# A hybrid decoder layer on one core: activation rows of 268 columns, other orders around two norms, three shifted feed-forward pairs

## The chip, the cores and the metric

The kernel runs on one core of one Trainium2 chip. The metric is the device time of one execution in microseconds. Work is shared by five engines, each with its own queue in program order: TensorE (PE; its weight loads are shown apart as PEld), VectorE (DVE), ScalarE (ACT), GpSimd (POOL) and SyncE (SP). They wait for each other on semaphores alone.

## The reference

One inference step of one decoder layer, for 256 prompt tokens and 8 sample tokens, 264 columns in all, in fp32:

```python
# token mixer: pooling branch, Mamba-2 SSD branch, gated merge, output projection
x = layer_norm(ALPHA * x + mix, ln_mix_g, ln_mix_b)
# cross-attention of 4 heads over 256 memory tokens
x = layer_norm(ALPHA * x + ca, ln_mem_g, ln_mem_b)
f = (silu(x @ w_ffn_gate) * (x @ w_ffn_up)) @ w_ffn_down      # 2048 -> 5632 -> 2048
x = layer_norm(ALPHA * x + f, ln_ffn_g, ln_ffn_b)

def layer_norm(x, g, b):
    mu = mean(x); var = mean((x - mu) ** 2)
    return (x - mu) * rsqrt(var + 1e-5) * g + b
```

It also returns the new SSD, convolution and pooling states and the memory keys and values.

## The kernel before

**Layout.** Activations are feature-major: a partition holds one feature of each of 16 tiles, and the columns are the 264 tokens. Every fp32 product is made of three matmuls on split operands: the rounded high part and the rest of the weights (`whi`, `wlo`) and of the activations (`xH`, `xL` for the layer's input `x`; `yH`/`yL`, `mixH`/`mixL`, `hH`/`hL` for the SSD output, the mixed branches and the hidden layer). `mm3` (L360 to L364) issues high x high (L362), high weights x low activations (L363) and low weights x high activations (L364).

**The weight stream.** All weights come as 688 units of 128 x 1024 fp32 (512 KB) through a ring of four slots. For each unit SP loads `raw` once the slot's last split is done, ACT's `split` writes `whi` (L807) once PE has finished the unit four before, DVE's `split` writes `wlo` (L1293) as `raw - whi`, and PE's `unit` waits for `wlo` and issues 24 matmuls: four tiles of the activations (`kk` 0 to 3), for each two output banks of three matmuls, so six matmuls in a row read the same tile. ACT and DVE can stand at most four units ahead of PE. Because every engine works in program order, a `split` that stands behind something that waits also waits, and so does PE's unit.

**Rows.** `xH` and `xL` hold 16 rows (one per tile) of T + 2 = 266 fp32 values in each partition, 1064 bytes from row to row; the two columns behind the 264 tokens are for the norm's gain and bias. `yH`, `mixH` and `hH` have rows of 264 values, 1056 bytes.

**The first norm** (`n` = 0, behind `w_out`). DVE adds the residual per block of two tiles (L1702, L1704), ACT squares it, DVE adds sums and squares, PE sums them over partitions (L601). Then for four chunks `c` of four tiles each: DVE's `ln_scale` (L1788, L1789: times the reciprocal deviation, plus the shifted mean), ACT's `ln_affine` (L1055, four activations: gain and bias), ACT's `ln_high` (L1062, writes `xH`), DVE's `ln_low` (L1793, writes `xL`). PE meanwhile makes the memory keys from `memH` (8 units, L623 and L624), and then the queries (8 units), which read `xH` and `xL` chunk by chunk.

**The second norm** (`n` = 1, behind `w_mo`, one unit per block of two tiles). Here the next matrix product starts before the norm's statistics are there: `gain_high` and `gain_low` write gain x residual into `xH` and `xL`, the first two feed-forward pairs run on these with 266 columns (the last two give the products with gain and bias), and DVE's `fix` (L1883, L1885) and `up_fixed` put deviation and mean in afterwards. A pair is one gate block and one up block of 4 units each, 8 units; there are 22 pairs. In the shadow of the two pairs DVE and ACT also make the true normed `x` (`ln_scale`, `ln_affine`), and write it over `xH` and `xL` (`ln_high`, `ln_low`) as PE leaves the chunks. Pairs 3 to 18 also carry the update of the sample states (`states`, `outers`).

**PSUM.** `SETS` are four pairs of banks: 0 and 1 are G, 2 and 3 are M. The blocks of `w_mo` go to sets 0, 1, 2 in turn; every pair has its gate in set 0 and its up in set 1. The sums of norm 1 use set 3.

## Time and profile before

| | |
|---|---|
| median of 3 runs | 2254.7 us (2253.25 to 2259.2) |
| the profiled execution's own time | 2259.79 us |
| its span | 2257.9 us |
| mean granted TensorE clock | 0.979 |
| PE busy | 2188.8 us, 97%, 17470 matmuls |
| PEld busy | 2161.8 us, 96% |
| DVE busy | 1465.7 us, 65% |
| ACT busy | 1138.8 us, 50% |
| POOL busy | 157.5 us, 7% |
| chain that ended last | PE 89%, DVE 6%, ACT 2%, DMA 2% |
| DMA | 451.75 MB, mean 200 GB/s |

The span runs from the first to the last instruction; 1.9 us of the profiled execution lie outside it. The busy share of PE counts matmuls whose spans overlap (a matmul takes about 0.29 us, and the next starts about 0.12 us after it), so what tells the pace is the distance from start to start. The clock of a stretch is the share of full speed that was granted: 1.00 is 2.4 GHz, and half of it 1.2 GHz.

### The profile page before, as it was taken

How to read it: one execution, taken by the hardware profiler on the slowest of the kernel's cores; microseconds unless marked ns; L12 is line 12 of the kernel's file. 1: busy time of each engine (PE TensorE's matmuls, PEld its weight loads, DVE VectorE, ACT ScalarE, POOL GpSimd, SP SyncE). 2: the span in 40 equal slices, each digit the busy share in tenths (PEclk: the TensorE clock that was granted, in tenths of full speed). 3: DMA queues.
4: the chain of work that ended last, by engine and by line, in shares of the span. 5: the costliest groups of instructions: out<-in, count | busy, mean ns of one | idle time of the engine just before them, and what ended most of it. 6: DMA issues, size and time to landing. Idle time of an engine off the chain costs nothing.

```text
span 2257.9 us, 47795 instructions
## 1 busy us (share of the span) xinstructions
PE 2188.8 (97%) x17470; PEld 2161.8 (96%) x17470; DVE 1465.7 (65%) x2336; ACT 1138.8 (50%) x1668; POOL 157.5 (7%) x295
## 2 busy tenths in 40 slices
PE   7999999999999998999999999989999999999995
PEld 6999999999999998999999999989999999999995
DVE  6688877888778887444446742876666665444444
ACT  4666566566545444343444542566656564443333
POOL 1000000000003331000000000001111110000000
PEclk9999999999999999999999987999999999999998
DMA  6555555455457997455556643358888886555552
GB/s 253 170 182 177 184 180 175 158 179 175 159 187 255 304 293 222 151 178 181 178 176 215 232 151 122 122 187 280 284 273 276 284 272 216 177 180 183 179 178 76
DMA packets 123104, 451.75 MB, mean 200 GB/s; under 512 B 15928, under 2 KB 16056, under 8 KB 121464
## 3 DMA queue, kind: packets, MB, share of 16 engines
q1 hardware_dynamic: 99648, 362.92, 46.6%
q0 software_dynamic: 23376, 87.69, 12.4%
q8 instruction: 59, 0.97, 0.2%
q14 instruction: 21, 0.17, 0.0%
HBM read 427.87 MB, written 23.99 MB: 200 GB/s over the span
## 4 chain that ended last, share of the span: by engine, by line
PE 89%; DVE 6%; ACT 2%; DMA 2%; issue 1%; SPq 0%; POOL 0%; DVEq 0%; ACTq 0%; POOLq 0%
PE G L362 24%; PE G L363 24%; PE G L364 24%; PE M L362 3%; PE M L363 3%; PE M L364 3%; DVE sb_wlo L1293 2%; DMA sb_raw<-in_wstream 1%; ACT sb_whi L807 1%; PE G L662 1%; PE M L449 1%; PE G L637 1%; PE M L459 1%; DVE sb_resid L1789 1%; DVE sb_resid L1788 1%
## 5 line engine op out<-in xcount | busy, mean ns | idle before, releaser
L1293 DVE TENSOR_TENSOR sb_wlo<-sb_raw,sb_whi 128x1024 fp32r<-128x1024 f32 x688 | 836.7, 1224 | 699.8 <-ACT sb_whi L807 698.6
L807 ACT ACTIVATE sb_whi<-sb_raw 128x1024 fp32r<-128x1024 f32 x688 | 723.1, 1058 | 809.5 <-PE G L364 662.2
L362 PE MATMUL G<-sb_xH,sb_whi 128*128 128x264 f32 (+1 forms) x3136 | 906.5, 289 | 29.3 <-DVE sb_wlo L1293 21.5
L363 PE MATMUL G<-sb_xL,sb_whi 128*128 128x264 f32 (+1 forms) x3136 | 902.7, 288 | 0.0
L364 PE MATMUL G<-sb_xH,sb_wlo 128*128 128x264 f32 (+1 forms) x3136 | 902.3, 288 | 0.0
L362 PEld LDWEIGHTS G<-sb_xH,sb_whi 128*128 128x128 f32 x3136 | 600.2, 191 | 36.6 <-issue 24.0
L363 PEld LDWEIGHTS G<-sb_xL,sb_whi 128*128 128x128 f32 x3136 | 599.5, 191 | 0.1
L364 PEld LDWEIGHTS G<-sb_xH,sb_wlo 128*128 128x128 f32 x3136 | 597.6, 191 | 0.0
L363 PE MATMUL G<-sb_hL,sb_whi 128*128 128x264 f32 x704 | 200.4, 285 | 0.0
L364 PE MATMUL G<-sb_hH,sb_wlo 128*128 128x264 f32 x704 | 200.1, 284 | 0.0
L362 PE MATMUL G<-sb_hH,sb_whi 128*128 128x264 f32 x704 | 199.5, 283 | 0.0
L362 PE MATMUL G<-sb_yH,sb_whi 128*128 128x264 f32 x512 | 146.8, 287 | 7.2 <-DVE sb_yL L1669 7.2
L363 PE MATMUL G<-sb_yL,sb_whi 128*128 128x264 f32 x512 | 146.9, 287 | 0.0
L364 PE MATMUL G<-sb_yH,sb_wlo 128*128 128x264 f32 x512 | 146.6, 286 | 0.0
L362 PEld LDWEIGHTS G<-sb_hH,sb_whi 128*128 128x128 f32 x704 | 132.6, 188 | 0.0
L364 PEld LDWEIGHTS G<-sb_hH,sb_wlo 128*128 128x128 f32 x704 | 132.5, 188 | 0.0
L363 PEld LDWEIGHTS G<-sb_hL,sb_whi 128*128 128x128 f32 x704 | 132.3, 188 | 0.0
L362 PE MATMUL M<-sb_xH,sb_whi 128*128 128x264 f32 x384 | 113.1, 295 | 4.0 <-DVE sb_xL L1793 4.0
L363 PE MATMUL M<-sb_xL,sb_whi 128*128 128x264 f32 x384 | 111.0, 289 | 0.0
L364 PE MATMUL M<-sb_xH,sb_wlo 128*128 128x264 f32 x384 | 111.0, 289 | 0.0
L362 PEld LDWEIGHTS G<-sb_yH,sb_whi 128*128 128x128 f32 x512 | 97.5, 190 | 7.3 <-issue 7.3
L364 PEld LDWEIGHTS G<-sb_yH,sb_wlo 128*128 128x128 f32 x512 | 97.2, 190 | 0.0
(355 smaller groups left out, 3002.0 us busy)
## 6 DMA issues: line engine op xcount, KB each, us to landing
sb_raw<-in_wstream SPq DMA_DIRECT2D x688, 512.0 KB, 3.5
sb_st<-in_state_ssd POOLq DMA_DIRECT2D x32, 512.0 KB, 6.1
out_new_ssd_s<-sb_st POOLq DMA_DIRECT2D x32, 512.0 KB, 3.3
sb_tmp<-in_state_ssd POOLq DMA_DIRECT2D x34, 256.0 KB, 5.1
sb_cumbc<-scr_cum POOLq DMA_DIRECT2D x8, 1024.0 KB, 4.9
...
```

The costliest lines, as they stand in the source:

```text
L362: pe.matmul(out, w, kH, start=start, stop=False)
L363: pe.matmul(out, w, kL, start=False, stop=False)
L364: return pe.matmul(out, wlo[:, slot, col:col + P], kH, start=False, stop=stop)
L449: pe.matmul(out, xdt[:, 0, h * 64:h * 64 + 64], MM[:, h % 3, 0:SEQ], start=True, stop=False)
L459: last = pe.matmul(M[2][:, j * P:j * P + P], xdt[:, b, j * P:j * P + P], Btok[:, b, :], start=b == 0, stop=b == 1)
L637: last = pe.matmul(X[:, c:c + 1], kc[:, h, b, m * P:m * P + P], qT[:, h, SEQ + b:SEQ + b + 1], start=True, stop=True)
L662: last = pe.matmul(X[:, 384 + c:385 + c], vc[:, h, b, m, :], sPT[:, m, c:c + 1], start=m == 0, stop=m == 1)
L807: act.activation(whi[:, slot, :], raw[:, slot, :], ACT.Copy).then_inc(hi_ready, 1)
L1293: dve.tensor_tensor(wlo[:, slot, :], raw[:, slot, :], whi[:, slot, :].bitcast(F32), ALU.subtract)\
L1788: step(dve.tensor_tensor(chunk(c), chunk(c), spread(RSTD[n]), ALU.mult))
L1789: dve.tensor_tensor(chunk(c), chunk(c), spread(MEAN[n]), ALU.add).then_inc(s["zn_ready"], 1)
```

## The change

Four things. (1) `xH` and `xL` get rows of T + 4 = 268 values, 1072 bytes; the small table `rc` moves into an overlay to make room. (2) First norm: DVE does three of the last block's four splits ahead of its residual instead of four, and the first `ln_scale` to `ln_low` are put in another order among the splits; ACT does the first chunk's affine and high part before the first keys. (3) Second norm: the first pair has its gate in set 2 and its up in set 0, the second in sets 1 and 2, and a third pair runs on the shifted residual in sets 0 and 1; the sums over partitions come behind the first gate's fourth unit instead of the third; DVE leaves the last tiles' sums and the last squares until after the last gain. (4) `ln_scale`, `ln_affine`, `ln_high` and `ln_low` of the second norm are spread over three pairs instead of two, so that one pair fewer follows the states.

The diff, without its parts that only change the signatures of `columns`, `fix` and `up_fixed` (each gets the pair of banks as an argument):

```diff
-        xH = alloc(ctx, "xH", [P, KT, T + 2], F32R)
-        xL = alloc(ctx, "xL", [P, KT, T + 2], F32R)
+        xH = alloc(ctx, "xH", [P, KT, T + 4], F32R)
+        xL = alloc(ctx, "xL", [P, KT, T + 4], F32R)
...
-        rc = alloc(ctx, "rc", [P, 4, 16])
+        (rc,) = overlay(KEEP + 3 * XPG * SG * 4 + 3 * P * 4, rc=([P, 4, 16],))
...
-            def pair(between=None, **kw):
+            def pair(gate, up, ready=None, between=None, n=T):
 
                 pe.wait_ge(s["sgm"], START["sgm"] + t["sgm"].now())
-                block_units(xH, xL, KT, SETS[0], between=between, **kw)
-                kw.pop("before", None)
+                block_units(xH, xL, KT, SETS[gate], n=n, before=ready, between=between)
                 pe.wait_ge(s["h_read"], START["h_read"] + t["h_read"].now())
-                block_units(xH, xL, KT, SETS[1], **kw)
+                block_units(xH, xL, KT, SETS[up], n=n)
                 t["sgm"].add(2)
                 t["h_read"].add(2)
 
-            pe.wait_ge(s["res_ready"], 8 + 7)
-            pair(n=T + 2, before=lambda q: pe.wait_ge(s["gd_lo"], 4 * (q + 1)), between=lambda q: ln_folded(1) if q == 2 else None)
-            pair(n=T + 2)
-            with rounds(pe, FT // 2 - 2, t, dict(unit=8, sgm=2, h_read=2)):
-                pair(before=lambda q: pe.wait_ge(s["x_lo"], 8 + q + 1))
+            pe.wait_ge(s["res_ready"], 8 + 6)
+            pair(2, 0, n=T + 2, ready=lambda q: pe.wait_ge(s["gd_lo"], 4 * (q + 1)),
+                 between=lambda q: ln_folded(1) if q == 3 else None)
+            pair(1, 2, n=T + 2)
+            pe.wait_ge(s["h_read"], START["h_read"] + 2)
+            pair(0, 1, n=T + 2)
+            with rounds(pe, FT // 2 - 3, t, dict(unit=8, sgm=2, h_read=2)):
+                pair(0, 1, ready=lambda q: pe.wait_ge(s["x_lo"], 8 + q + 1))
...
             ln_squares(0, 7)
-            split(2)
+            split(1)
             ln_mean(0)
             split(1)
             ln_sd(0)
             split(1)
+            ln_affine(0, 0)
+            ln_high(0, 0)
+            split(1)
             keys(0)
-            for c in range(4):
+            for c in (1, 2, 3):
                 ln_affine(0, c)
                 ln_high(0, c)
-                split(1)
+                split(1 if c < 3 else 2)
             keys(1)
...
+            split(4)
+            ln_mean(1)
+            ln_sd(1)
+            columns(0, 2)
+            split(1)
+            silu_fixed(0)
+            split(1)
+            ln_affine(1, 0)
             split(2)
-            ln_mean(1)
-            split(1)
-            ln_sd(1)
-            columns(0)
-            split(1)
-            silu_fixed(0)
-            ln_affine(1, 0)
-            split(1)
+            columns(1, 0)
+            hidden_high()
+
+            split(2)
             ln_affine(1, 1)
             split(2)
-            columns(1)
-            split(1)
+            ln_affine(1, 2)
+            columns(0, 1)
+            split(1)
+            silu_fixed(1)
+            split(3)
+            ln_affine(1, 3)
+            columns(1, 2)
             hidden_high()
 
-            split(2)
-            ln_affine(1, 2)
-            split(2)
-            columns(0)
-            silu_fixed(1)
-            ln_affine(1, 3)
+            split(4)
+            columns(0, 0)
+            silu_fixed(2)
             for c in range(4):
                 split(1)
                 act.wait_ge(used, t["done"].now() + c + 1 + RING)
                 ln_high(1, c)
-            columns(1)
+            columns(1, 1)
             hidden_high()
 
...
-                split(4)
+                split(4 if b < 7 else 3)
...
             ln_rstd(0)
             ln_scale(0, 0)
             split(1)
-            for c in range(4):
-                if c < 3:
-                    ln_scale(0, c + 1)
-                split(1)
-                ln_low(0, c)
+            ln_scale(0, 1)
+            split(1)
+            ln_low(0, 0)
+            split(1)
+            ln_scale(0, 2)
+            ln_low(0, 1)
+            split(1)
+            ln_scale(0, 3)
+            ln_low(0, 2)
+            split(2)
+            ln_low(0, 3)
             split(8)
...
-                if b:
+                if 0 < b < 7:
                     add_tiles(1, b)
-                if b >= 2:
+                if 2 <= b < 7:
                     add_squares(1, b - 1)
                 if b:
                     gain_low(b - 1)
+            gain_low(7)
+            split(1)
+            add_tiles(1, 7)
+            add_squares(1, 6)
             add_squares(1, 7)
-            gain_low(7)
             fold(1)
 
...
             ln_variance(1)
             split(1)
             ln_rstd(1)
-            split(1)
-            fix(0, sgF)
+            fix(0, 2, sgF)
+            split(1)
             ln_scale(1, 0)
+            split(3)
+            up_fixed(0)
+            hidden_low()
+
             split(1)
             ln_scale(1, 1)
-            split(3)
-            up_fixed()
-            hidden_low()
-
             split(2)
             ln_scale(1, 2)
-            split(2)
-            fix(0, sgF)
+            split(1)
+            fix(0, 1, sgF)
+            split(1)
             ln_scale(1, 3)
+            split(3)
+            up_fixed(2)
+            hidden_low()
+
+            split(4)
+            fix(0, 0, sgF)
             for c in range(4):
                 split(1)
                 if c == 3:
-                    up_fixed()
+                    up_fixed(1)
                 ln_low(1, c)
             hidden_low()
 
```

What stands where, before and after. In these rows `sb_wlo` is a split of DVE, `sb_resid<-sb_resid,sb_lrstd` and `sb_resid<-sb_resid,sb_mean` are the two halves of `ln_scale`, and `sb_xL<-sb_resid,sb_xH` is `ln_low`.

DVE in the first norm, from the scale of chunk 1 to the low part of chunk 2, before:

```order
L1788 TENSOR_TENSOR sb_resid<-sb_resid,sb_lrstd 128x1056
L1789 TENSOR_TENSOR sb_resid<-sb_resid,sb_mean 128x1056
L1293 TENSOR_TENSOR sb_wlo<-sb_raw,sb_whi 128x1024
L1793 TENSOR_TENSOR sb_xL<-sb_resid,sb_xH 128x4x264
L1788 TENSOR_TENSOR sb_resid<-sb_resid,sb_lrstd 128x1056
L1789 TENSOR_TENSOR sb_resid<-sb_resid,sb_mean 128x1056
L1293 TENSOR_TENSOR sb_wlo<-sb_raw,sb_whi 128x1024
L1793 TENSOR_TENSOR sb_xL<-sb_resid,sb_xH 128x4x264
L1788 TENSOR_TENSOR sb_resid<-sb_resid,sb_lrstd 128x1056
L1789 TENSOR_TENSOR sb_resid<-sb_resid,sb_mean 128x1056
L1293 TENSOR_TENSOR sb_wlo<-sb_raw,sb_whi 128x1024
L1793 TENSOR_TENSOR sb_xL<-sb_resid,sb_xH 128x4x264
```

The same stretch of DVE after the change:

```order
L1799 TENSOR_TENSOR sb_resid<-sb_resid,sb_lrstd 128x1056
L1800 TENSOR_TENSOR sb_resid<-sb_resid,sb_mean 128x1056
L1304 TENSOR_TENSOR sb_wlo<-sb_raw,sb_whi 128x1024
L1804 TENSOR_TENSOR sb_xL<-sb_resid,sb_xH 128x4x264
L1304 TENSOR_TENSOR sb_wlo<-sb_raw,sb_whi 128x1024
L1799 TENSOR_TENSOR sb_resid<-sb_resid,sb_lrstd 128x1056
L1800 TENSOR_TENSOR sb_resid<-sb_resid,sb_mean 128x1056
L1804 TENSOR_TENSOR sb_xL<-sb_resid,sb_xH 128x4x264
L1304 TENSOR_TENSOR sb_wlo<-sb_raw,sb_whi 128x1024
L1799 TENSOR_TENSOR sb_resid<-sb_resid,sb_lrstd 128x1056
L1800 TENSOR_TENSOR sb_resid<-sb_resid,sb_mean 128x1056
L1804 TENSOR_TENSOR sb_xL<-sb_resid,sb_xH 128x4x264
```

Counting the units of the stream from the first of the memory keys as 0, the two splits shown first are units 8 and 9 before and 7 and 8 after: unit 8 now stands between the low part of chunk 0 and the scale of chunk 2, and unit 9 between the low part of chunk 1 and the scale of chunk 3.

ACT from the standard deviation of the first norm to the high part of chunk 1 (`sb_KTm` are keys, `sb_resid<-sb_resid,sb_vec` is the affine, `sb_xH` the high part), before:

```order
L1045 ACTIVATE sb_lrstd<-sb_lrstd,sb_eps 128x264
L807 ACTIVATE sb_whi<-sb_raw 128x1024
L1083 ACTIVATE sb_KTm<-G 128x256 x2
L1055 ACTIVATE sb_resid<-sb_resid,sb_vec 128x264 x4
L1062 ACTIVATE sb_xH<-sb_resid 128x4x264
L807 ACTIVATE sb_whi<-sb_raw 128x1024
L1055 ACTIVATE sb_resid<-sb_resid,sb_vec 128x264 x4
L1062 ACTIVATE sb_xH<-sb_resid 128x4x264
```

And after:

```order
L1047 ACTIVATE sb_lrstd<-sb_lrstd,sb_eps 128x264
L809 ACTIVATE sb_whi<-sb_raw 128x1024
L1057 ACTIVATE sb_resid<-sb_resid,sb_vec 128x264 x4
L1064 ACTIVATE sb_xH<-sb_resid 128x4x264
L809 ACTIVATE sb_whi<-sb_raw 128x1024
L1085 ACTIVATE sb_KTm<-G 128x256 x2
L1057 ACTIVATE sb_resid<-sb_resid,sb_vec 128x264 x4
L1064 ACTIVATE sb_xH<-sb_resid 128x4x264
```

The keys come after the first chunk. The two splits shown are units 7 and 8 before, and 6 and 7 after: each unit from 8 on now stands behind the high part of one chunk later (unit 8 behind chunk 1, unit 9 behind chunk 2, units 10 and 11 behind chunk 3), where before it stood behind chunks 0, 1, 2 and 3.

DVE at the end of the blocks of `w_mo`, from the last block's residual on (`sb_xL<-sb_resid,sb_vec,sb_xH` is `gain_low`, `sb_sums` are the sums of tiles and squares), before:

```order
L1707 SCALAR_TENSOR_TENSOR sb_resid<-sb_resid,G 128x528
L1729 TENSOR_TENSOR sb_sums<-sb_sums,sb_resid 128x528
L1741 TENSOR_TENSOR sb_sums<-sb_sums,sb_squares 128x528
L1853 SCALAR_TENSOR_TENSOR sb_xL<-sb_resid,sb_vec,sb_xH 128x264 x2
L1741 TENSOR_TENSOR sb_sums<-sb_sums,sb_squares 128x528
L1853 SCALAR_TENSOR_TENSOR sb_xL<-sb_resid,sb_vec,sb_xH 128x264 x2
L1748 TENSOR_TENSOR sb_sums<-sb_sums 128x264 x2
L1293 TENSOR_TENSOR sb_wlo<-sb_raw,sb_whi 128x1024 x2
```

And after:

```order
L1718 SCALAR_TENSOR_TENSOR sb_resid<-sb_resid,G 128x528
L1870 SCALAR_TENSOR_TENSOR sb_xL<-sb_resid,sb_vec,sb_xH 128x264 x4
L1304 TENSOR_TENSOR sb_wlo<-sb_raw,sb_whi 128x1024
L1740 TENSOR_TENSOR sb_sums<-sb_sums,sb_resid 128x528
L1752 TENSOR_TENSOR sb_sums<-sb_sums,sb_squares 128x528 x2
L1759 TENSOR_TENSOR sb_sums<-sb_sums 128x264 x2
L1304 TENSOR_TENSOR sb_wlo<-sb_raw,sb_whi 128x1024 x2
```

The gains and one split stand ahead of the last sums.

## Rows read from the trace of the kernel before

**Rows 1.** The page's first line.

```profile
span 2257.9 us, 47795 instructions
```

**Rows 2.** What PE waited for, 1275:1315 us: us in total, times, longest.

```profile
PE M L362 <- DVE sb_xL L1793: 4.0, 3, 1.6
PE G L601 <- DVE sb_sums L1748: 0.8, 1, 0.8
```

**Rows 3.** The same view, 1410:1512 us.

```profile
PE G L362 <- DVE sb_xL L1793: 3.9, 1, 3.9
PE G L362 <- DVE sb_resid L1707: 3.8, 1, 3.8
PE G L362 <- DVE sb_wlo L1293: 3.3, 1, 3.3
```

**Rows 4.** Windows: busy (x instructions) of PE, PEld, DVE, ACT, POOL; clock; DMA, GB/s.

```profile
1530.00:1700.00 170.00, 170.00 (x1384) 170.00 (x1383) 113.74 (x199) 102.00 (x199) 23.57 (x44) 1.00 0.82 278
1970.00:2100.00 130.00, 130.00 (x1072) 129.93 (x1070) 60.32 (x56) 50.16 (x52) 0.00 (x0) 1.00 0.54 180
```

**Rows 5.** Windows, instructions that touch `sb_xH` alone, whole span (no POOL).

```profile
0.00:2258.00 2258.00, 1336.05 (x7040) 1118.31 (x7040) 28.09 (x38) 20.60 (x30) 0.98 0.59 200
```

**Rows 6.** Timeline of PE: start, us; each sixth matmul, rows 6 to 11.

```profile
1610.04 0.29 PE L362 MATMUL G<-sb_xH,sb_whi 128*128 128x264 f32 x1
...
1610.79 0.28 PE L362 MATMUL G<-sb_xH,sb_whi 128*128 128x264 f32 x1
...
1611.53 0.28 PE L362 MATMUL G<-sb_xH,sb_whi 128*128 128x264 f32 x1
...
1612.24 0.28 PE L362 MATMUL G<-sb_xH,sb_whi 128*128 128x264 f32 x1
...
1612.99 0.29 PE L362 MATMUL G<-sb_xH,sb_whi 128*128 128x264 f32 x1
...
1613.72 0.29 PE L362 MATMUL G<-sb_xH,sb_whi 128*128 128x264 f32 x1
...
1614.46 0.28 PE L362 MATMUL G<-sb_xH,sb_whi 128*128 128x264 f32 x1
```

**Rows 7.** Timeline of DVE in the first norm, one round.

```profile
1299.28 1.22 DVE L1293 TENSOR_TENSOR sb_wlo<-sb_raw,sb_whi 128x1024 fp32r<-128x1024 f32 x1
1300.42 1.25 DVE L1793 TENSOR_TENSOR sb_xL<-sb_resid,sb_xH 128x1056 fp32r<-128x1056 f32 x1
1301.58 1.25 DVE L1788 TENSOR_TENSOR sb_resid<-sb_resid,sb_lrstd 128x1056 f32<-128x1056 f32 x1
1302.87 1.26 DVE L1789 TENSOR_TENSOR sb_resid<-sb_resid,sb_mean 128x1056 f32<-128x1056 f32 x1
1304.05 1.22 DVE L1293 TENSOR_TENSOR sb_wlo<-sb_raw,sb_whi 128x1024 fp32r<-128x1024 f32 x1
```

**Rows 8.** Timeline of ACT there.

```profile
1299.40 2.10 ACT L1055 ACTIVATE sb_resid<-sb_resid,sb_vec 128x264 f32<-128x264 f32 x4 [0.86 <-DVE sb_resid L1789]
1301.53 1.09 ACT L1062 ACTIVATE sb_xH<-sb_resid 128x1056 fp32r<-128x1056 f32 x1
1302.53 1.04 ACT L807 ACTIVATE sb_whi<-sb_raw 128x1024 fp32r<-128x1024 f32 x1
```

**Rows 9.** Windows at two of the second norm's stalls, columns as in rows 4.

```profile
1436.00:1444.00 8.00, 6.47 (x30) 6.47 (x31) 7.93 (x13) 3.60 (x7) 0.00 (x0) 0.57 0.39 131
1470.00:1475.00 5.00, 3.58 (x18) 3.58 (x19) 4.83 (x6) 2.05 (x4) 0.00 (x0) 0.66 0.44 132
```

**Rows 10.** Timeline of DVE and ACT at the last two blocks of `w_mo`.

```profile
1436.78 0.70 DVE L1707 SCALAR_TENSOR_TENSOR sb_resid<-sb_resid,G 128x528 f32<-128x528 f32 x1
...
1440.70 0.70 DVE L1707 SCALAR_TENSOR_TENSOR sb_resid<-sb_resid,G 128x528 f32<-128x528 f32 x1
...
1441.43 0.64 ACT L1036 ACTIVATE sb_squares<-sb_resid 128x528 f32<-128x528 f32 x1 [2.47 <-DVE sb_resid L1707]
1441.98 0.91 ACT L1164 ACTIVATE sb_xH<-sb_resid,sb_vec 128x264 fp32r<-128x264 f32 x2
...
1444.11 0.89 DVE L1853 SCALAR_TENSOR_TENSOR sb_xL<-sb_resid,sb_vec,sb_xH 128x264 fp32r<-128x264 f32 x2
```

18 lines of the change are left out of this document (9 added, 9 removed).

## The prediction

> **What bounds the kernel now.** I read four views. The page first: the span is 2257.9 us [rows 1], and its chain of waits lies mostly in PE's own matmuls, so the time is the sum of PE's steps and its stalls. Next, what PE waited for, by stretch. Two of the stretches with stalls are where the order changes: in the first norm PE stands idle 4.0 us in three waits for low parts of `x` and 0.8 us for the sums [rows 2]; in the second 3.9, 3.8 and 3.3 us, one wait each, for the low part of chunk 0, for the last-but-one residual and for a weight split [rows 3], 11.0 us in all. Then the windows for the pace: where PE never stalls and reads `xH` and `xL`, 1384 matmuls fill 170 us, 122.8 ns each; over the hidden layer, 1072 fill 130 us, 121.3 ns [rows 4]. Last, the timeline of both norms, for what each wait waits on.
>
> **Rows of 1072 bytes.** The change adds no matmul; it moves where a row of `xH` and `xL` begins. With three arrays of 16,384 bytes ahead of them, row k begins at 1064k bytes: even rows on a multiple of 16, odd rows 8 bytes off. In one stall-free stretch each row is read by six matmuls. Rows 6 to 11 take, start to start, 0.75, 0.74, 0.71, 0.75, 0.73 and 0.74 us [rows 6]: the even ones 0.730 on average, the odd ones 0.743, or 121.7 and 123.9 ns per matmul. That is one sample at a resolution of 10 ns, but the pace of the hidden layer, all of whose rows are multiples of 32 bytes, points the same way. At 1072 bytes every row begins on a multiple of 16. Two estimates: half the matmuls lose 2.2 ns, 1.1 ns on average; or all fall to the hidden layer's pace, 1.5 ns. The even rows of 1064 are not alike themselves: row 6, 48 bytes past a multiple of 64, takes 0.75, as slow as any odd row, and with 1072 a quarter of the rows begin so instead of an eighth. I take 0.85 ns. `xH` is read by 7040 matmuls [rows 5], two of every three, so 10,560 are touched: 10,560 x 0.85 ns = 9.0 us less. The bounds are 10,560 x 1.5 = 15.8 us less, and nothing. DVE and ACT touch `xH` in 38 and 30 instructions in all [rows 5]; a few ns in these don't reach PE.
>
> The Trainium skill bears on this from both sides. Its page "SBUF — State Buffer" (Specifications (TRN2)) gives 16-byte cachelines, with a penalty for each crossing to a new line; a row of 264 fp32 values that begins 8 bytes off crosses one line more. The page "TensorE: Matmul & The Clock Gate" (Back-to-back issue gap) sets the spacing of a stream by the matmul's columns and the weight load together, with no word of where a row begins; by it the pace would not change, which is the first rival below. The difference between rows 6 to 11 leans to the first page.
>
> **The first norm.** What goes: DVE no longer does the fourth split ahead of the last residual, so the sums come about a split (1.1 us) earlier, and the 0.8 us wait for them [rows 2] ends. What is late next is the splits of units 8 to 10 of the stream, counted from the first of the memory keys; units 8 to 11 are the first queries. Before, ACT split unit 8 behind chunk 0, 9 behind chunk 1, 10 behind chunk 2, and the scale of chunk 1 was done before DVE came to unit 8, so a round was bounded by DVE alone: one unit every 4.77 us (1299.28 to 1304.05) [rows 7]. PE needs 2.96 us for a unit (24 x 123 ns), which leaves a wait of some 1.3 us behind each. After, ACT's split of unit 9 stands behind the affine and high part of chunk 2, these wait for DVE's scale of chunk 2, and that stands behind DVE's split of unit 8, which itself waits for ACT behind chunk 1. So a round is a chain with no overlap: DVE's split 1.14 (1299.28 to 1300.42), scale 1.29 + 1.26 = 2.55 [rows 7], ACT's affine 2.13, high part 1.00, split 1.04 [rows 8], and a few hand-overs of some 0.05: 7.95 us. It occurs twice, for units 9 and 10; unit 11 follows unit 10 at once. PE waits 7.95 - 2.96 = 5.0 us twice, and about 0.4 at unit 8, since that split now follows chunk 1. New stalls 10.4, old 4.0 + 0.8: 5.6 us more, and I take 5.5. Behind the waiting splits on DVE stand the low parts of chunks 1 and 2; those are later too, but within the same waits.
>
> Such stalls cost clock besides. In the second norm, behind stalls of 3.3 to 3.9 us, the granted clock is 0.57 over 8 us and 0.66 over 5 us, part of the time at 1.2 GHz [rows 9], which loses 8 x 0.43 = 3.4 us and 5 x 0.34 = 1.7 us against 2.4 GHz. Stalls of up to 1.6 us in the first norm show no such thing. Behind the first 5.0 us stall the loss is hidden: a unit at half clock takes at most 2 x 2.96 = 5.9 us and the chain 7.95. Behind the second it is not: 1.7 to 3.4, I take 2.5. The bounds of this part: if the chain overlapped after all, 0.8 less than before; if both stalls cost 3.4 us of clock in the open, 5.6 + 6.8 = 12.4 more.
>
> **The second norm.** Three stalls of 11.0 us [rows 3] and three losses of clock, 3.4 + 1.7 + 1.7 (the third stall's window reads like the second's) = 6.8 us; 17.8 us is all there is.
> The wait for the residual (3.8): PE's first gate goes to set 2, free since the residual of block 5. DVE's residuals come 3.92 us apart (1436.78, 1440.70) [rows 10], so that of block 5 began at about 1432.9, and PE starts the gate about 3.7 us sooner, at 1433.8. Its fourth unit needs the last gain: the last residual stays at 1440.7, ACT squares it at 1441.43 (0.64 from issue) and makes the gain's high part from 1441.98 (0.91), DVE's low part takes 0.89 and stands ahead of everything else now, so it ends at 1443.8 instead of 1445.0 [rows 10]. PE has done three units by 1433.8 + 8.9 = 1442.7: it waits 1.2. The sums' tail on DVE (split 1.1, tiles 0.6, two squares 1.2, fold 0.7) ends at 1447.4, and the fourth unit at 1446.9: 0.6.
> The wait for the split (3.3): it came from a scale, an affine and a split in turn between ACT and DVE inside one pair. Now two or more splits stand between such chains everywhere but ahead of the third pair, where DVE's scale of chunk 3 (2.5 us) stands before its second unit: 0.3 + 0.65 there.
> The wait for the low part (3.9): the last scale and affine were done only as PE left the chunk. With a third pair they lie a pair earlier, and high and low parts of chunks 0 to 3 take 3.4 us a chunk between the two engines against PE's 2.96 per unit, started 6 us ahead: no wait.
> What is left is 1.2 + 0.6 + 0.95 = 2.8 us. A third pair with 266 columns instead of 264 costs 192 matmuls x 1 ns = 0.2. So 17.8 - 2.8 - 0.2 = 14.8 us less. If 1.2 and 0.6, so close together, cost a window of clock (1.7 us), 13.1; I allow half of that, 0.8. Bounds: 11, if another wait of the old size (3.8) comes in place of one, and 17.8.
>
> **The rest** costs nothing: `rc` is read in the pooling stage, which is loaded long before; a pair fewer behind the states leaves three, 72 us, for their last stores, which PE never waits for; the tail and the attention stage are the same.
>
> **The sum**, against the profiled execution's own 2259.8 us (its span 2257.9 and 1.9 around it): -9.0 + 5.5 + 2.5 - 14.8 + 0.8 = -15.0, so 2244.8. The median is 2254.7, 5.1 below that execution, so 2239.7; I say 2240.
>
> **The rivals.** (a) The row's start buys nothing: the 2.2 ns between odd and even rows would be their place in the unit, which doesn't change. For it: row 6 is as slow as the odd ones. Against it: the pace over the hidden layer is 1.5 ns better with the same places. The time: 2240 + 9 = 2249. (b) No chain in the first norm, because ACT comes through earlier than I reckon: 5.5 + 2.5 + 0.8 less, 2231. For it: ACT's first chunk stands ahead of the keys now. Against it: the order of both queues. (c) The second norm keeps one stall of the old size with its clock, at the third or fourth pair: 3.8 + 1.7 more, 2245. (d) Slower: what sets the pace is not 16 bytes but how a row lies in 64, or the distance between rows, and 1072 is the worse one. The slowest rows now take 0.75 us for six, 125 ns, 2.2 more than the pace of 122.8; if all did, 10,560 x 2.2 = 23.2 us more, and with the norms as above 2254.7 + 23.2 + 5.5 + 2.5 - 14 = 2272. It decides, with a kernel over 0.3% slower, from 12.8 us lost on, a pace of 124.0. For it: row 6. Against it: rows 8 and 10, at 0 and 16 bytes past, with 0.71 and 0.73 [rows 6].
>
> **How the numbers follow.** My forecast 70%, with 2232 to 2247 as its own range; (a) 12%, (b) 8%, (c) 6%, (d) 4%. The range that holds 8 in 10 is 2230 to 2249. A measurement of this kernel can tell 0.3%, 6.8 us, from no change: faster means below 2247.9. All of (b) and (c), nearly all of the forecast and a fifth of (a) lie there: 86%; within 0.3% most of (a) and the forecast's upper edge, 10%; slower (d), 4%.
>
> **What would show it.** The pace over `xH` near 122.0 ns in the window of 170 us (about 1393 matmuls where 1384 were), and no difference left between odd and even rows; the pace over the hidden layer as before. In the first norm two waits of PE for `sb_wlo`, near 5 us each, with the clock below 1 behind the second. In the second norm no wait over 1.5 us. Wrong would be: a pace over `xH` still at 122.8; waits in the first norm of 2 us or less; a wait over 3 us for `sb_xL` or `sb_wlo` in the pairs.

## The result, and the profile after

| | before | after |
|---|---|---|
| median | 2254.42 us (2253.25 to 2259.2, 4 runs) | 2227.95 us (2226.09 to 2229.49, 4 runs) |
| profiled execution | 2259.79 us | 2226.51 us |
| span | 2257.9 us | 2225.0 us |

The changed kernel is faster by 26.5 us, a ratio of 0.9878 [0.9861, 0.9896]. The forecast was 2240 with a range down to 2230: the direction came as written and so did what happens in both norms, the size did not, and the time fell below the range. The two profiled executions lie 33.0 us of span apart, more than the medians, because the one of before was about 5 us above its median and the one of after 1.4 below. Two single executions, one of 3531 us with only `xL` at 1072 bytes and one of 2653 us with the first norm alone, fell far out of their kernels' spread at a much lower granted clock and are left out of the medians and ratios below.

The page of after, its first line, the busy times and the chain that ended last (the line that answers to [rows 1] is the first):

```profile
span 2225.0 us, 47769 instructions
...
PE 2159.8 (97%) x17470; PEld 2133.2 (96%) x17470; DVE 1469.3 (66%) x2342; ACT 1138.6 (51%) x1670; POOL 157.4 (7%) x295
...
PE 89%; DVE 5%; DMA 2%; ACT 2%; issue 1%; SPq 0%; POOL 0%; DVEq 0%; ACTq 0%; POOLq 0%
```

PE's matmuls are as many as before and still make the chain. To see where 33.0 us went, I took from PE's timeline of both kernels the start of certain units of the weight stream (us; unit 392 is the first of the memory keys, 404 the fifth of the queries, 416 the first of `w_mo`, 424 the first of pair 0, 448 the first of pair 3, 600 the first of `w_ffn_down`):

| stretch | before | after | difference |
|---|---|---|---|
| start to 392, no edit but the rows | 1272.36 | 1260.09 | -12.3 |
| 392 to 404, first norm | 41.52 | 46.59 | +5.1 |
| 404 to 416, queries 5 to 8, values, attention | 92.07 | 89.26 | -2.8 |
| 416 to 448, `w_mo` and three pairs | 116.97 | 101.21 | -15.8 |
| 448 to 600, nineteen pairs | 448.90 | 441.81 | -7.1 |
| 600 to the end | 286.12 | 286.02 | -0.1 |

One profile of each kernel is not exact to a microsecond or two in such a stretch: the time at 1.2 GHz in the first row, for one, is 17.1 us before and 13.7 after. The repeat of the changed kernel below shows how far it moves.

**The pace.** Windows of after over the stretches of [rows 4]; the columns are the same:

```profile
1530.00:1700.00 170.00, 170.00 (x1406) 170.00 (x1406) 115.06 (x208) 104.93 (x209) 23.23 (x44) 1.00 0.83 281
1970.00:2100.00 130.00, 130.00 (x1071) 129.93 (x1070) 60.81 (x55) 48.57 (x48) 0.00 (x0) 1.00 0.54 180
```

In 170 us without a stall 1406 matmuls stand where 1384 were; 1393 were forecast. Over the hidden layer, whose rows weren't touched, nothing moves: 1071 against 1072. Sixteen pairs without a stall (units 456 to 584, 3072 matmuls) give the sharper number: 378.02 us before, 372.05 after, which is 123.05 and 121.11 ns per matmul, 1.94 ns less. The timeline of PE, each sixth matmul, answers to [rows 6]:

```profile
1610.49 0.28 PE L362 MATMUL G<-sb_xH,sb_whi 128*128 128x264 f32 x1
...
1611.22 0.29 PE L362 MATMUL G<-sb_xH,sb_whi 128*128 128x264 f32 x1
...
1611.95 0.28 PE L362 MATMUL G<-sb_xH,sb_whi 128*128 128x264 f32 x1
...
1612.68 0.29 PE L362 MATMUL G<-sb_xH,sb_whi 128*128 128x264 f32 x1
```

The three rows shown take 0.73 us each, where odd and even ones took 0.74 and 0.73 on average before, with single ones from 0.71 to 0.75. Over the same sixteen pairs, each row read 32 times: even rows took 122.0 ns per matmul before and 121.1 after, odd rows 124.1 and 121.1. Single rows still differ after the change, from 119.4 ns (row 3) to 124.2 (row 2), though all begin on a multiple of 16. This pattern over the 16 rows is the same to 0.1 ns in all seven profiles with rows of 1072 bytes, and another one is the same in all four with 1064.

**The first norm.** What PE waited for, 1265:1320 us of after, against [rows 2]:

```profile
PE M L362 <- DVE sb_wlo L1304: 9.0, 3, 4.8
```

Three waits, 9.0 us, where 4.8 were. The timeline of PE has each of them:

```profile
1284.94 0.36 PE L362 MATMUL M<-sb_xH,sb_whi 128*128 128x264 f32 x1 [0.77 <-DVE sb_wlo L1304]
...
1292.85 0.56 PE L362 MATMUL M<-sb_xH,sb_whi 128*128 128x264 f32 x1 [4.77 <-DVE sb_wlo L1304]
...
1300.77 0.36 PE L362 MATMUL M<-sb_xH,sb_whi 128*128 128x264 f32 x1 [3.47 <-DVE sb_wlo L1304]
```

They stand 7.91 and 7.92 us apart, start to start. Why, the timelines of DVE and then of ACT say (a bracket is the idle time ahead of the instruction and who ended it):

```profile
1283.56 1.23 DVE L1304 TENSOR_TENSOR sb_wlo<-sb_raw,sb_whi 128x1024 fp32r<-128x1024 f32 x1 [2.20 <-ACT sb_whi L809]
1284.71 1.25 DVE L1799 TENSOR_TENSOR sb_resid<-sb_resid,sb_lrstd 128x1056 f32<-128x1056 f32 x1
1285.99 1.26 DVE L1800 TENSOR_TENSOR sb_resid<-sb_resid,sb_mean 128x1056 f32<-128x1056 f32 x1
1287.17 1.25 DVE L1804 TENSOR_TENSOR sb_xL<-sb_resid,sb_xH 128x1056 fp32r<-128x1056 f32 x1
1291.48 1.23 DVE L1304 TENSOR_TENSOR sb_wlo<-sb_raw,sb_whi 128x1024 fp32r<-128x1024 f32 x1 [3.06 <-ACT sb_whi L809]
```

```profile
1287.29 2.10 ACT L1057 ACTIVATE sb_resid<-sb_resid,sb_vec 128x264 f32<-128x264 f32 x4 [3.75 <-DVE sb_resid L1800]
1289.42 1.08 ACT L1064 ACTIVATE sb_xH<-sb_resid 128x1056 fp32r<-128x1056 f32 x1
1290.41 1.04 ACT L809 ACTIVATE sb_whi<-sb_raw 128x1024 fp32r<-128x1024 f32 x1
```

Read across both: split on DVE, its two scales, then ACT's affine (idle 3.75 us until then), high part and split, then DVE again (idle 3.06 us until then). Neither engine does anything beside the other but one low part. From one split to the next it is 1283.56 to 1291.48, 7.92 us; [rows 7, 8] had given 7.95.

**The second norm.** What PE waited for, 1400:1512 us of after, against 11.0 us in [rows 3]:

```profile
PE M L601 <- DVE sb_sums L1759: 1.0, 1, 1.0
PE M L362 <- DVE sb_xL L1870: 0.5, 1, 0.5
PE G L362 <- DVE sb_wlo L1304: 0.3, 1, 0.3
PE M L572 <- DVE sb_resid L1718: 0.2, 1, 0.2
```

And the windows: the clock behind the first norm's long wait, the attention, and the whole of the second norm.

```profile
1290.00:1296.00 6.00, 3.15 (x15) 3.18 (x16) 4.48 (x4) 2.25 (x4) 0.00 (x0) 0.72 0.25 86
...
1330.11:1395.94 65.83, 64.85 (x439) 62.61 (x437) 19.90 (x38) 20.77 (x46) 1.59 (x3) 0.82 0.39 133
1410.00:1512.00 102.00, 100.12 (x803) 99.03 (x802) 88.40 (x115) 62.70 (x100) 2.12 (x4) 1.00 0.53 174
```

Over the second norm the granted clock is 1.00 throughout, where [rows 9] had 0.57 and 0.66.

### The profile page after: what moved, and what is told of

It is laid out like the page before. It is cut to its first block, busy times and chain, and to the rows that moved or that the text cites. A ratio compares the mean times of both kernels' runs of the same rounds, so it can differ in the third digit from the quotient of the medians.

```text
span 2225.0 us, 47769 instructions
## 1 busy us (share of the span) xinstructions
PE 2159.8 (97%) x17470; PEld 2133.2 (96%) x17470; DVE 1469.3 (66%) x2342; ACT 1138.6 (51%) x1670; POOL 157.4 (7%) x295
## 4 chain that ended last, share of the span: by engine, by line
PE 89%; DVE 5%; DMA 2%; ACT 2%; issue 1%; SPq 0%; POOL 0%; DVEq 0%; ACTq 0%; POOLq 0%
PE G L362 24%; PE G L363 24%; PE G L364 24%; PE M L362 3%; PE M L363 3%; PE M L364 3%; DVE sb_wlo L1304 2%; DMA sb_raw<-in_wstream 2%; PE M L449 1%; ACT sb_whi L809 1%; PE G L662 1%; PE G L637 1%; PE M L459 1%; ACT sb_resid L1057 1%; DVE sb_resid L1800 0%
## 5 line engine op out<-in xcount | busy, mean ns | idle before, releaser
L362 PE MATMUL G<-sb_xH,sb_whi 128*128 128x264 f32 (+1 forms) x3072 | 880.5, 287 | 19.9 <-DVE sb_wlo L1304 19.9
L364 PE MATMUL G<-sb_xH,sb_wlo 128*128 128x264 f32 (+1 forms) x3072 | 875.7, 285 | 0.0
L363 PE MATMUL G<-sb_xL,sb_whi 128*128 128x264 f32 (+1 forms) x3072 | 875.4, 285 | 0.0
L362 PEld LDWEIGHTS G<-sb_xH,sb_whi 128*128 128x128 f32 x3072 | 581.9, 189 | 26.8 <-issue 20.7
L363 PEld LDWEIGHTS G<-sb_xL,sb_whi 128*128 128x128 f32 x3072 | 581.6, 189 | 0.1
L364 PEld LDWEIGHTS G<-sb_xH,sb_wlo 128*128 128x128 f32 x3072 | 581.3, 189 | 0.0
L363 PE MATMUL G<-sb_hL,sb_whi 128*128 128x264 f32 x704 | 200.4, 285 | 0.0
L364 PE MATMUL G<-sb_hH,sb_wlo 128*128 128x264 f32 x704 | 200.0, 284 | 0.0
L362 PE MATMUL G<-sb_hH,sb_whi 128*128 128x264 f32 x704 | 199.5, 283 | 0.0
L362 PE MATMUL G<-sb_yH,sb_whi 128*128 128x264 f32 x512 | 146.6, 286 | 7.2 <-DVE sb_yL L1680 7.2
L363 PE MATMUL G<-sb_yL,sb_whi 128*128 128x264 f32 x512 | 146.6, 286 | 0.0
L364 PE MATMUL G<-sb_yH,sb_wlo 128*128 128x264 f32 x512 | 146.3, 286 | 0.0
L362 PE MATMUL M<-sb_xH,sb_whi 128*128 128x264 f32 (+1 forms) x448 | 132.1, 295 | 9.5 <-DVE sb_wlo L1304 9.0
L362 PEld LDWEIGHTS G<-sb_hH,sb_whi 128*128 128x128 f32 x704 | 132.6, 188 | 0.0
L364 PEld LDWEIGHTS G<-sb_hH,sb_wlo 128*128 128x128 f32 x704 | 132.5, 188 | 0.0
L363 PEld LDWEIGHTS G<-sb_hL,sb_whi 128*128 128x128 f32 x704 | 132.2, 188 | 0.0
L363 PE MATMUL M<-sb_xL,sb_whi 128*128 128x264 f32 (+1 forms) x448 | 129.8, 290 | 0.0
L364 PE MATMUL M<-sb_xH,sb_wlo 128*128 128x264 f32 (+1 forms) x448 | 129.7, 289 | 0.0
L362 PEld LDWEIGHTS G<-sb_yH,sb_whi 128*128 128x128 f32 x512 | 97.4, 190 | 7.3 <-issue 7.3
L362 PEld LDWEIGHTS M<-sb_xH,sb_whi 128*128 128x128 f32 x448 | 87.0, 194 | 10.8 <-issue 9.5
```

The lines of the kernel that those rows point to most:

```text
L362: pe.matmul(out, w, kH, start=start, stop=False)
L363: pe.matmul(out, w, kL, start=False, stop=False)
L364: return pe.matmul(out, wlo[:, slot, col:col + P], kH, start=False, stop=stop)
```

## The experiments

The question after the result was: does the row's start give twice what I took, or does something else in the change give it? And do the other two parts cost and give what their rows say? Each part was done alone and undone alone.

**Rows alone.** Kernel before, with rows of 1072 bytes and `rc` moved, as in the change.

```diff
-        xH = alloc(ctx, "xH", [P, KT, T + 2], F32R)
-        xL = alloc(ctx, "xL", [P, KT, T + 2], F32R)
+        xH = alloc(ctx, "xH", [P, KT, T + 4], F32R)
+        xL = alloc(ctx, "xL", [P, KT, T + 4], F32R)
-        rc = alloc(ctx, "rc", [P, 4, 16])
+        (rc,) = overlay(KEEP + 3 * XPG * SG * 4 + 3 * P * 4, rc=([P, 4, 16],))
```

> The kernel before with nothing changed but the rows of xH and xL (268 columns, 1072 bytes) and the place of rc. Theory A: the start of a row on a multiple of 16 bytes sets the pace; in the changed kernel the pace over xH was 121.4 ns where it was 122.95, so 10,560 x 1.55 ns = 16.4 us less than before (2238), about 1406 matmuls in the window 1530:1700 instead of 1384, and the waits of both norms as before (4.0 + 0.8 and 11.0 us). Theory B (my prediction's size): 0.85 ns, 9 us less (2245.5). Rival: the pace fell because of something else in the changed kernel (fewer stalls, other transfers), then 2254 and 122.9 ns here.

Measured: 2239.65 us (2235.36 to 2240.87) against 2257.72 of the kernel before on the same chip, ratio 0.9918 [0.9897, 0.9939], which is 18.5 us (13.8 to 23.3). The window of 170 us:

```profile
1530.00:1700.00 170.00, 170.00 (x1406) 170.00 (x1405) 114.07 (x204) 104.13 (x206) 23.54 (x44) 1.00 0.83 283
```

The full 1406 matmuls are there, and the stalls of both norms are those of before. So the rows alone give 18.5 us, about two thirds of the whole gain, and my 9.0 falls.

**Rows back.** Kernel after, rows of 1064 bytes again.

```diff
-        xH = alloc(ctx, "xH", [P, KT, T + 4], F32R)
-        xL = alloc(ctx, "xL", [P, KT, T + 4], F32R)
+        xH = alloc(ctx, "xH", [P, KT, T + 2], F32R)
+        xL = alloc(ctx, "xL", [P, KT, T + 2], F32R)
```

> The changed kernel with rows of 266 columns again, all else as changed. Theory A: the pace returns to 122.9 ns over xH and the time rises by 16 us over the changed kernel, to about 2244; even and odd rows differ by 2 ns again. Theory B: 9 us, 2237. The stalls of both norms stay as in the changed kernel (9 us and 2 us).

Measured: 2246.17 us (2242.83 to 2250.25), ratio 0.9952 [0.9936, 0.9968]: against the changed kernel's 0.9878 that is 0.0074, some 17 us. (`rc` stays where the change put it, so its move isn't what gives the time.) Its window:

```profile
1530.00:1700.00 170.00, 170.00 (x1384) 170.00 (x1383) 112.38 (x198) 102.51 (x202) 23.64 (x44) 1.00 0.83 278
```

1384 matmuls again. Done or undone, the part is worth the same within the noise, so it does not depend on the rest.

**Rows of 1068 bytes.** Kernel after. Row k then begins 0, 12, 8 or 4 bytes past a multiple of 16, in turn.

```diff
-        xH = alloc(ctx, "xH", [P, KT, T + 4], F32R)
-        xL = alloc(ctx, "xL", [P, KT, T + 4], F32R)
+        xH = alloc(ctx, "xH", [P, KT, T + 3], F32R)
+        xL = alloc(ctx, "xL", [P, KT, T + 3], F32R)
```

> The changed kernel with rows of 267 columns, 1068 bytes: only every fourth row begins on a multiple of 16, the others 4, 8 or 12 bytes off. Theory A (each row off a multiple of 16 costs its six matmuls about 3.9 ns each, from 1.94 ns on average at half the rows off): three quarters off, 121.1 + 2.9 = 124.0 ns over xH, 10,560 x 2.9 = 31 us over the changed kernel, 2259. Rival 1 (only 8 bytes off costs): a quarter off, 122.1 ns, 10 us over. Rival 2 (it is the pitch of 1064 bytes and not the row's start): 121.1 ns and no change.

Measured: 2247.56 us (2244.79 to 2250.76), ratio 0.996 [0.9947, 0.9974], some 21 us slower than the changed kernel in the same session (its repeat below).

```profile
1530.00:1700.00 170.00, 170.00 (x1388) 170.00 (x1387) 111.77 (x199) 101.95 (x199) 23.48 (x44) 1.00 0.82 278
```

1388 in the window; 122.71 ns per matmul over the sixteen pairs, where I had written 124.0, 122.1 or 121.1: none of the three came. A count of rows off 16 would have made it worse than 1064 (three of four off instead of one of two), and it is a shade better. By row, from PE's timeline over the same pairs, the means are 122.3 ns at 0 bytes, 120.7 at 12, 124.2 at 8 and 123.7 at 4. In the changed kernel, with all of them aligned, the same rows take 121.0, 121.6, 121.2 and 120.6. So rows 8 and 4 bytes off are slower by 3 ns, the aligned ones by 1.3, and rows 12 off are faster by 0.9. Which row is 12 off is also always the second tile of a unit; but that place isn't a fast one, it is the slowest of the four when all are aligned. What these means can't show is which matmul a cost belongs to, if it comes out in a neighbour, and each is of four rows only, where single aligned rows differ by up to 4.8 ns. The Trainium skill ("SBUF — State Buffer", Specifications (TRN2)) counts a penalty for each crossing into a new 16-byte cacheline; a row of 1056 bytes crosses one line more at any start that isn't a multiple of 16. The trace agrees for 4 and 8 bytes (123.7 and 124.2 against 122.3 ns) and not for 12 (120.7).

**Only `xL` at 1072 bytes.** Kernel after, `xH` at 1064.

```diff
-        xH = alloc(ctx, "xH", [P, KT, T + 4], F32R)
+        xH = alloc(ctx, "xH", [P, KT, T + 2], F32R)
```

> The changed kernel with xH at 266 columns again and only xL at 268: one matmul in three reads aligned rows. Theory A (each read of a row off a multiple of 16 pays for itself): the changed kernel gains 1.94 ns per matmul over the pitch of 1064, so a third of it is left, 122.4 ns over xH and 12 us over the changed kernel. Rival (the cost arises between two reads, from one row's start to the next one's, so that a mixed order is no better): 123.0 ns, 18 to 20 us over.

Measured: 2237.6 us (2234.97 to 2241.05) against 2258.83, ratio 0.99 [0.9885, 0.9915], by the ratios 5 to 7 us slower than the changed kernel.

```profile
1530.00:1700.00 170.00, 170.00 (x1396) 170.00 (x1395) 114.26 (x204) 103.25 (x206) 23.56 (x44) 1.00 0.83 280
```

The pace is 121.94 ns, so 1.11 of the 1.94 ns are won, 57%, where only one matmul in three reads `xL`. It meets neither expectation: a saving of an equal share for each matmul that reads an aligned row would be a third. Either a matmul of `xL` gains 3.3 ns itself, or one beside it gains with it. PE's timeline tells: each product is issued as `xH`, `xL`, `xH` (L362, L363, L364), and from the start of each to the next start the means over the sixteen pairs are

| from the start of | before | only `xL` | changed |
|---|---|---|---|
| L362, reads `xH` | 122.6 | 122.6 | 121.1 |
| L363, reads `xL` | 123.0 | 121.4 | 120.9 |
| L364, reads `xH` | 123.5 | 121.8 | 121.4 |

With only `xL` aligned, the matmul that reads it gains 1.6 ns and the one behind it 1.7, though that one still reads `xH` as before; the one ahead of it gains nothing. So what `xL` costs off 16 comes out in two matmuls, the reader and the next. Why, no run shows.

**First norm put back.** Kernel after, with ACT's and DVE's old orders in the first norm.

```diff
-            split(1)
+            split(2)
...
-            ln_affine(0, 0)
-            ln_high(0, 0)
-            split(1)
...
-            for c in (1, 2, 3):
+            for c in range(4):
...
-                split(1 if c < 3 else 2)
+                split(1)
...
-                split(4 if b < 7 else 3)
+                split(4)
...
-            ln_scale(0, 1)
-            split(1)
-            ln_low(0, 0)
-            split(1)
-            ln_scale(0, 2)
-            ln_low(0, 1)
-            split(1)
-            ln_scale(0, 3)
-            ln_low(0, 2)
-            split(2)
-            ln_low(0, 3)
+            for c in range(4):
+                if c < 3:
+                    ln_scale(0, c + 1)
+                split(1)
+                ln_low(0, c)
```

> The changed kernel with the first norm's orders on ACT and DVE as before (four splits ahead of the last residual, keys ahead of the first chunk, one scale, split and low part in turn). Theory A (the chain of scale, affine, high part, split and split costs 5.6 us less 0.5, and some clock behind it): the waits for wlo in the first norm (4.8 + 3.5 + 0.8) go, three waits for xL of 1.1 to 1.6 us come back, the queries start 5 us earlier, and the time is 5 to 8 us under the changed kernel, about 2222. Rival: the attention stage is held by something else (transfers, its own clock), and the time stays within 2 us of 2228.

Measured: 2225.81 us (2221.98 to 2228.69), ratio 0.9856 [0.9835, 0.9876], by the ratios 5 us under the changed kernel (0.9878) and 3 under its repeat (0.987), with intervals that overlap both. What PE waited for is [rows 2] again:

```profile
PE M L362 <- DVE sb_xL L1801: 4.0, 3, 1.6
PE G L601 <- DVE sb_sums L1756: 0.8, 1, 0.8
```

The stretch 392 to 404 takes 41.5 us, 5.1 less than in the changed kernel. But the next, 404 to 416, takes 93.5 instead of 89.3. So the waits behave as I said, and part of what they cost comes back in the next stretch.

**First norm alone.** Kernel before, with the new orders; in ACT's queue (and DVE's, as in the change):

```diff
-            split(2)
+            split(1)
...
+            ln_affine(0, 0)
+            ln_high(0, 0)
+            split(1)
...
-            for c in range(4):
+            for c in (1, 2, 3):
...
-                split(1)
+                split(1 if c < 3 else 2)
```

> The kernel before with the first norm's part of the change alone. Theory A: two waits for wlo of about 4.7 us, 392 to 404 takes 47 to 49 us instead of 41.5, and the attention stage behind it gives back about 3 us, because less of it falls to 1.2 GHz: 2 to 4 us over the kernel before, hardly to be told from no change. Rival: the attention stage gives nothing back, 6 to 8 us over it.

Measured: 2262.1 us (2259.58 to 2265.95) against 2258.83, ratio 1.0017 [1.0008, 1.0027], 3.8 us slower (1.8 to 6.1).

```profile
PE M L362 <- DVE sb_wlo L1296: 8.2, 3, 4.7
```

8.2 us of waits in place of 4.8, and 392 to 404 takes 48.8 us, 7.3 more; 404 to 416 takes 85.7, 6.3 less than in the profile of before. This part costs, but less than its waits.

**The changed kernel again**, with no edit.

> The changed kernel once more, beside the next three on one chip. All theories: 26 to 30 us under the kernel before. In its profile unit 392 to 404 of the stream (the first norm) 46.6 us, 416 to 448 (the second) 101 us; the attention stage between them, 404 to 416, anything from 85 to 94 us, by where the stretches at 1.2 GHz fall, if these differ from execution to execution (theory A); or 89.3 us again, if they are fixed by the kernel (rival).

Measured: 2226.32 us (2224.98 to 2233.26) against 2257.11, ratio 0.987 [0.9853, 0.9887], which is 29 us where the first comparison had 26.5. Its profile gives 48.9 us for 392 to 404 and 91.3 for 404 to 416, where the first gave 46.6 and 89.3. One kernel, two profiles, 2 us apart in each stretch. Windows of the attention (units 408 to 416), in three fences: of before, of the first norm alone, and of this run.

```profile
1335.87:1405.95 70.08, 69.10 (x438) 66.81 (x437) 19.90 (x38) 20.76 (x46) 1.59 (x3) 0.76 0.37 131
```

```profile
1340.64:1407.42 66.78, 65.81 (x438) 63.50 (x437) 19.90 (x38) 20.75 (x46) 1.59 (x3) 0.80 0.42 146
```

```profile
1329.51:1398.95 69.44, 68.46 (x438) 65.90 (x437) 19.90 (x38) 20.78 (x46) 1.59 (x3) 0.76 0.38 132
```

The work is the same to the instruction. Time multiplied by clock: 70.08 x 0.76 = 53.3, 66.78 x 0.80 = 53.4, 69.44 x 0.76 = 52.8, and in the window of after above 65.83 x 0.82 = 54.0. What differs is the share of the stretch at 1.2 GHz. Summed over 404 to 416, the time at 1.2 GHz is 40.8 us in the profile of before, 34.1 in that of after, 39.5 in this run, 44.5 with the first norm put back and 26.9 with the first norm alone.

**ACT's splits ahead of the affine.** Kernel after; in ACT's queue alone each split of the first norm moves from behind a chunk's affine and high part to ahead of it.

```diff
-            split(1)
+            split(2)
             ln_affine(0, 0)
...
             for c in (1, 2, 3):
+                split(1)
                 ln_affine(0, c)
                 ln_high(0, c)
-                split(1 if c < 3 else 2)
```

> The changed kernel with DVE's order untouched and one split of ACT moved: two splits ahead of the first chunk's affine, and the others ahead of their chunk instead of behind it. Theory A (each split on ACT that stood behind a chunk's high part waited for DVE's scale, which stood behind DVE's split of the unit before): the chain opens, one wait of about 1 us for wlo is left of 9, and the time is 8 to 10 us under the changed kernel, about 2219. Rival: DVE's order alone (a split ahead of the scales of chunks 2 and 3) makes the chain; then the waits of 4.8 and 3.5 us stay and the time is 2228.

Measured: 2220.58 us (2218.99 to 2222.18), ratio 0.9838 [0.9821, 0.9855]. PE's waits in the first norm:

```profile
PE M L362 <- DVE sb_wlo L1304: 2.3, 1, 2.3
```

And ACT's timeline in place of the one above:

```profile
1285.36 1.06 ACT L809 ACTIVATE sb_whi<-sb_raw 128x1024 fp32r<-128x1024 f32 x1
1286.31 2.10 ACT L1057 ACTIVATE sb_resid<-sb_resid,sb_vec 128x264 f32<-128x264 f32 x4
1288.44 1.09 ACT L1064 ACTIVATE sb_xH<-sb_resid 128x1056 fp32r<-128x1056 f32 x1
1289.43 1.04 ACT L809 ACTIVATE sb_whi<-sb_raw 128x1024 fp32r<-128x1024 f32 x1
```

The affine has no idle time before it, where it had 3.75 us. DVE's order is that of the changed kernel. So moving ACT's splits is enough to open the chain, and DVE's order alone doesn't make it. No run put DVE's order back and left ACT's, so whether that would open it too isn't shown.

**The same kernel once more**, beside the runs of other parts on another chip.

> The changed kernel with one split of ACT moved ahead, once more: 2219 to 2221, 36 us under the kernel before, about 6 to 8 under the changed one. If its lead was an accident of where the slow clock fell, 2226.

Measured: 2223.85 us (2220.62 to 2224.55) against 2258.83, ratio 0.984 [0.9826, 0.9853]. Of the kernels here it is the fastest: 1.6% under the kernel before both times, and by the ratios 7 to 9 us under the changed one (0.9838 and 0.984 against 0.9878 and 0.987). Its two profiles lie as far apart as any: 404 to 416 takes 85.4 us in the first and 91.5 in the second, with 26.6 and 39.8 us of it at 1.2 GHz.

**Second norm alone.** Kernel before, with that part of the change only: the same edits as in the diff ahead of the prediction (sets, third shifted pair, late sums, the spread of scales and affines), rows of 1064 bytes, first norm as before; only `rc` is moved as well.

```diff
-            pair(n=T + 2, before=lambda q: pe.wait_ge(s["gd_lo"], 4 * (q + 1)), between=lambda q: ln_folded(1) if q == 2 else None)
-            pair(n=T + 2)
...
+            pair(2, 0, n=T + 2, ready=lambda q: pe.wait_ge(s["gd_lo"], 4 * (q + 1)),
+                 between=lambda q: ln_folded(1) if q == 3 else None)
+            pair(1, 2, n=T + 2)
+            pe.wait_ge(s["h_read"], START["h_read"] + 2)
+            pair(0, 1, n=T + 2)
```

> The kernel before with the second norm's part of the change alone (set rotation, third pair, late sums; rows of 266 columns, first norm as before). Theory A: 416 to 448 takes 103 us where the kernel before takes 117, and the time is 13 to 15 us under the kernel before. Rival: the gain is only there together with the shorter rows' pace, under 8 us.

Measured: 2245.79 us (2242.79 to 2245.96), ratio 0.9949 [0.9935, 0.9962], 11.5 us less (8.6 to 14.7). Its stretch 416 to 448 takes 102.8 us where the profile of before had 117.0, and the clock is 1.00 over the norm itself (3.6 us at 1.2 GHz lie ahead of it, in the first blocks of `w_mo`):

```profile
1420.00:1506.00 86.00, 84.08 (x671) 83.09 (x671) 75.83 (x99) 53.06 (x83) 0.00 (x0) 1.00 0.50 170
```

**Two shifted pairs.** Kernel after without the third pair, with the sets' rotation and the late sums kept.

```diff
-            pe.wait_ge(s["h_read"], START["h_read"] + 2)
-            pair(0, 1, n=T + 2)
-            with rounds(pe, FT // 2 - 3, t, dict(unit=8, sgm=2, h_read=2)):
+            with rounds(pe, FT // 2 - 2, t, dict(unit=8, sgm=2, h_read=2)):
...
-            split(4)
-            columns(0, 0)
-            silu_fixed(2)
...
-            split(3)
-            up_fixed(2)
-            hidden_low()
-
-            split(4)
-            fix(0, 0, sgF)
...
+            split(1)
+            ln_scale(1, 1)
+            split(2)
```

ACT's and DVE's scales and affines stand inside two pairs again, as they did before.

> The changed kernel with two pairs on the shifted residual instead of three (gates in sets 2 and 1, ups in sets 0 and 2; sums late, as changed), DVE and ACT with the scales, affines, fixes and splits of the second norm in nearly the order of before. Theory A (the third pair is what takes two of the three stalls): a wait of about 4 us for xL at the third pair and one of about 3 for wlo in the second come back, each with 1.7 us of clock: 9 to 11 us over the changed kernel, about 2237. Rival (the freed set and the late sums do it all): under 3 us over it.

Measured: 2243.52 us (2237.03 to 2250.72), ratio 0.9943 [0.9922, 0.9963], some 17 us slower than the changed kernel in the same session, where 9 to 11 were expected; the executions spread widely, and by the two intervals it could be as little as 8. What PE waited for, 1410:1512 us:

```profile
PE G L362 <- DVE sb_xL L1794: 4.6, 1, 4.6
PE G L362 <- DVE sb_wlo L1294: 3.5, 1, 3.5
PE M L601 <- DVE sb_sums L1749: 1.0, 1, 1.0
PE M L362 <- DVE sb_wlo L1294: 0.7, 1, 0.7
PE M L362 <- DVE sb_xL L1860: 0.6, 1, 0.6
```

The waits for the low part and for the split are back (3.9 and 3.3 in [rows 3]); the one for the residual stays away. Units 424 to 448 take 88.1 us instead of 75.1, with 10.2 us of it at 1.2 GHz instead of none. So of the second norm's gain the third pair gives 12.9 us by the profiles, and the rotation and the late sums the rest, 1.3 us over units 416 to 448 (115.7 here against 117.0 before).

## Why the prediction was wrong in size and right in kind

**Rows: the step that failed is "I take 0.85 ns".** Measured are 1.94 ns over the pairs, and 18.5 us instead of 9.0. It was not only the choice between my two estimates: 1.1 and 1.5 ns and even the bound of 15.8 us were too small. Ahead of the first norm, over the 150 units of `xH` in which no matmul starts more than 0.15 us after the last, it is 1.70 ns (122.84 before, 121.14 after); 6144 matmuls there and 4416 behind make 10.4 + 8.6 = 19.0 us, which fits the 18.5.

The first estimate rested on the difference of 2.2 ns between odd and even rows, taken as the loss of odd rows alone. The reading was right (2.1 over the whole sixteen pairs), the step from it wasn't: odd rows gained 3.0 ns, and even rows, whose start is as good at 1064 bytes as at 1072, gained 0.9. More than half of that lies in the last of a row's six matmuls, whose next start is that of an odd row (123.6 before, 120.3 after; the other five 121.7 and 121.3). A difference between neighbours in one queue understates a cost that neighbours share. The second estimate, the distance to the hidden layer's pace, was nearer; with rows of 1072 bytes the pace went slightly below that of the hidden layer (121.1 against 121.3), so this pace was no floor.

Both estimates were then shaded down because row 6, 48 bytes past a multiple of 64, took 0.75 us. That reading was no accident either: row 6 is at 125.4 ns on average over the sixteen pairs. What was wrong is the cause that I gave it. Row 14, also 48 past, is at 121.8, and after the change the rows 0, 16, 32 and 48 bytes past are at 121.0, 120.6, 121.2 and 121.6. Single rows differ by several ns for a reason that no run shows, and it isn't their place in 64 bytes.

With 18.5 in place of 9.0 my sum gives 2230.2, and the rest of the miss is in the norms.

**First norm: the chain right, its price in the end too high.** The round was 7.92 us for 7.95. The waits were 0.8, 4.8 and 3.5 us for 0.4, 5.0 and 5.0; the third is shorter because the clock fell behind the first long wait (0.72 from 1290 to 1296) and PE was slower over that unit, which the round hid, as said. I took +8.0 us for waits and clock. In the profile of after the clock was 1.00 behind the second long wait and units 392 to 404 took 5.1 us more; in the other six profiles with these orders, 10.2 us of the stretch ran at 1.2 GHz and it took 6.0 to 7.4 us more. But end to end the part alone costs 3.8. I had written that the attention stage stays the same, and this is the other step that failed: units 404 to 416 took 91.9 to 93.5 us in the four profiles with the old orders and 85.7 to 91.3 in the seven with the new ones. So some of the price is given back there. Why is not shown. The time at 1.2 GHz in that stretch was anywhere from 27 to 45 us in thirteen profiles, and one kernel alone, the one with the splits moved, had 26.6 and 39.8.

**Second norm: right in the waits, some 2.5 us too high in the end.** The profiles gave 15.8 and, in the repeat, 13.6 us less over units 416 to 448, forecast 14.8 and 0.8 back for clock; the part alone gave 14.1. The extra 1.6 us of the first profile are clock and not the faster rows: it had no time at 1.2 GHz in the blocks of `w_mo`, where the part alone had 3.6 us and the repeat 4.8, and the three pairs take 75.1 us with rows of 1064 bytes as with 1072. Left waits 0.5, 1.0 and 0.3 us for 1.2, 0.6 and 0.95; no clock was lost. End to end the part alone gave 11.5, where I took 14.0. That the third pair removes the waits for the low part and the split was shown by taking it away.

**The rivals.** (a), that the row's start buys nothing, falls by the rows alone; 2.2 ns between odd and even rows was not their place, since it is gone at 1072 bytes. The spacing rule of the Trainium skill ("TensorE: Matmul & The Clock Gate", Back-to-back issue gap), which went with it, knows columns and weight loads only: at equal columns and loads the trace has 123.05 and 121.11 ns, so it doesn't hold to 2 ns. (b), no chain, falls by the timelines; the order that it described is the one that the moved ACT splits make. (c) falls: no wait above 1.0 us. (d), slower by the place in 64 bytes or the distance between rows, falls because the kernel isn't slower, and by the four classes above. One rival to my reading of the gain stands: in every run the distance between rows decides where they begin. No run moved the start and kept the distance.

The parts add up: -18.5, -11.5 and +3.8 are -26.2, against -26.5 measured and 29 in the repeat. Each part is known to 2 to 5 us only, so that they meet to 0.3 is luck; that they meet to a few us says that the parts don't need each other.

**Open.** Whether the start of a row or the distance between rows is the cause. Why rows 12 bytes off 16 aren't slow, why a neighbour shares the cost, and what makes aligned rows differ among themselves. What sets how long the attention runs at 1.2 GHz.
